# Projections interleaved with the state-space scan, keys turned in place, and a shared key copy in a one-core decoder layer

## The chip, the cores and the metric

The kernel runs on one core of a Trainium2 chip. The metric is the device time of one execution in microseconds (us). The kernel before took 1406.85 us (median of 3 runs, 1405.76 to 1408.14).

## The reference

One decoder layer on two inputs at once: a prompt of 256 tokens and 8 samples of 4 new tokens with a cache of 1024 positions. Everything is float32. Cut to what matters here:

```python
h = rmsnorm(x, norm_mix)
q, k, v, z, dt_raw, xbc = split(h @ w_in)            # 1024 -> 3080 columns
q, k = rope(rmsnorm(q)), rope(rmsnorm(k))            # 8 heads of 64
att = dilated_attention(q, k, v)                     # prompt: own keys; samples: cached keys and values too
u = silu(causal_conv(xbc, conv_w) + conv_b)          # width 4
xs, b_in, c_in = split(u)
dt = softplus(dt_raw + dt_bias)
y, h_last = ssd_scan(xs, dt, -exp(a_log), b_in, c_in, h0)   # chunks of 128 tokens, 8 heads
y = rmsnorm((y + xs * d_skip) * silu(z))
x = x + concat(att, y) @ w_out
x = x + memory_attend(rmsnorm(x), mem_k, mem_v) @ w_mem_o
x = x + moe_ffn(rmsnorm(x))                          # 32 experts, top 4, 12 MB of weights each
```

## The kernel before

It is one program of five instruction streams (TensorE, VectorE, ScalarE, GpSimd, and SyncE, which issues most transfers). Each stream is written out in order by hand, and streams meet only at named semaphores; nothing is reordered. So an engine that waits holds back all that stands behind it in its stream.

The 288 tokens are three row tiles: t = 0 and 1 are the prompt's halves (128 rows each), t = 2 is the 32 sample rows. Weights and caches come through a ring of six slots of 2 MB (`UNITS` assigns the slot, unit number modulo 6; `freed` says which semaphore frees it). SyncE loads the units in list order and waits for each slot in turn.

TensorE's stream up to the experts has these stages, each finished before the next begins:

1. Projections (L362 q, k, v, z for both halves, each into a bank of its own; L369 the samples; L377 dt; L389 the eight column tiles of xbc). ScalarE copies the results, VectorE norms and ropes q and k, then convolves xbc (L1104, L1106).
2. Prompt attention: q and k turned (L399, L407), the scores (L426), softmax on VectorE and ScalarE (L1144 to L1153, L1650), the probabilities turned (L463) and the values weighed (L474).
3. The scan, chunk by chunk: scores of the chunk (L511), decay sums (L517), initial states turned (L497), the part within a chunk (L544), the chunk's state (L552), and on the other engines the decay matrix (L1206, L1208 on VectorE, its exponential L1683 on ScalarE, L1212 on VectorE) and y (L1218 to L1241). GpSimd scales the initial states (L1890). Then the new sample states (L568, VectorE L1259), the norm of y and its turning (L582).
4. Window attention of the samples, in two batch groups g of four batches. For each pair of batches (bb) ten key tiles are turned (L601) into three banks and copied by ScalarE into `KTB` (L1699), and the scores run in two column groups of the array (L622). Then softmax, the probabilities turned (L629), the values weighed (L642), the rows selected (L648).
5. The output projection w_out (L662, L667), then the memory keys and values (L690, L704), memory attention and its projection, and the router, which ends at about 459 us. The expert loop follows: 32 experts through the same ring.

Stages 1 to 5 up to L704 are what the change touches. A float32 matmul shows as two MATMUL records, a transpose as one.

## Time and profile before

| | |
|---|---|
| median of 3 runs | 1406.85 us |
| the profiled execution's own time | 1409.51 us |
| its span, first to last instruction | 1407.3 us |
| TensorE busy | 1275.6 us, 91% |
| VectorE, ScalarE, GpSimd busy | 343.7, 268.3, 35.0 us |
| bytes read from memory | 463.94 MB |
| mean granted TensorE clock | 0.956 of full |

The page's shares are of the whole run, two thirds of which is the expert loop. What a change before the loop is worth is read from the stretches before it. "Busy" counts a matmul at the clock that was granted, so the same work counts up to twice as long at the lower of the two clock levels (1.2 and 2.4 GHz; a clock of 0.50 is all 1.2 GHz).

### The profile page before, as it was taken

Reading aid. Unit: us, or ns where it says so; the run is one execution under the profiler, and the core shown is the slowest. Engines: PE = TensorE matmul, PEld = TensorE weight load, DVE = VectorE, ACT = ScalarE, POOL = GpSimd, SP = SyncE. Lnnn points to the kernel's source line nnn. Section 1 sums busy time; section 2 is a strip of 40 time slices with the busy share of each in tenths; the row PEclk is TensorE's granted clock in tenths of the full one; section 3 lists DMA queues with packets and bytes.
Section 4 is the critical chain, followed back from the end, with each engine's and each line's share of the span. In section 5 each row is a group of like instructions: output and inputs, shape, how many; then the busy total and the mean of one; then the engine's idle time right before and its main releaser. Section 6 shows DMA issues by size and latency. Waiting matters only on the chain.

```text
span 1407.3 us, 15596 instructions
## 1 busy us (share of the span) xinstructions
PE 1275.6 (91%) x6333; PEld 519.7 (37%) x6333; DVE 343.7 (24%) x600; ACT 268.3 (19%) x520; POOL 35.0 (2%) x43
## 2 busy tenths in 40 slices
PE   6998788899778899999999999999999999999997
PEld 3467545344534233333323233232332323323232
DVE  1247550132405212212112121131211312113122
ACT  2126223310422110111102111021110211102111
POOL 0011320000000000000000000000000000000000
PEclk9998768999997899999999999999999999999999
DMA  9251028875028499999999999999999999999995
GB/s 343 103 198 49 0 78 317 312 268 203 12 74 344 154 409 432 426 431 426 431 426 431 426 430 427 430 427 430 427 430 427 430 427 431 426 430 427 430 427 217
DMA packets 54621, 470.19 MB, mean 334 GB/s; under 512 B 6417, under 2 KB 6673, under 8 KB 27972
## 3 DMA queue, kind: packets, MB, share of 16 engines
q1 hardware_dynamic: 52852, 463.69, 79.3%
q0 software_dynamic: 1744, 6.14, 1.4%
q8 instruction: 18, 0.29, 0.1%
q14 instruction: 7, 0.06, 0.0%
HBM read 463.94 MB, written 5.88 MB: 334 GB/s over the span
## 4 chain that ended last, share of the span: by engine, by line
PE 62%; DMA 23%; DVE 8%; ACT 6%; issue 1%; SPq 0%; ACTq 0%; DVEq 0%
DMA ring<-in_w_gate_up 23%; PE PS L913 22%; PE PS L945 10%; PE PS L893 5%; PE PS L362 4%; PE PS L662 3%; PE PS L389 2%; PE PS L704 2%; PE PS L622 1%; PE PS L716 1%; ACT arena L1699 1%; PE PS L642 1%; DVE arena L1503 1%; DVE arena L1505 1%; DVE arena L1500 1%
## 5 line engine op out<-in xcount | busy, mean ns | idle before, releaser
L913 PE MATMUL PS<-ring,arena 128*64 128x512 f32 x1792 | 406.2, 596 | 38.6 <-DMA ring<-in_w_gate_up 37.8
L913 PEld LDWEIGHTS PS<-ring,arena 128*64 128x64 f32 x1792 | 125.8, 137 | 307.1 <-issue 233.2
L945 PE MATMUL PS<-ring,arena 128*64 128x512 f32 x1024 | 230.3, 597 | 5.6 <-ACT arena L1817 5.6
L1500 DVE TENSOR_SCALAR arena<-PS 128x512 f32<-128x512 f32 x32 | 22.1, 692 | 425.9 <-PE PS L913 425.9
L1814 ACT ACTIVATE arena<-arena 128x512 f32<-128x512 f32 x32 | 20.1, 629 | 522.6 <-DVE arena L1500 522.6
L945 PEld LDWEIGHTS PS<-ring,arena 128*64 128x64 f32 x1024 | 69.3, 137 | 132.7 <-issue 118.8
L1466 DVE TENSOR_TENSOR X<-X,PS 128x1024 f32<-128x1024 f32 x34 | 41.5, 1221 | 272.2 <-PE PS L893 272.2
L872 PE MATMUL PS<-arena 128*64 128x512 f32 (+1 forms) x396 | 97.5, 610 | 2.2 <-issue 2.2
L893 PE MATMUL PS<-arena 128*64 128x512 f32 x340 | 81.3, 592 | 1.4 <-ACT arena L1824 1.4
L1824 ACT COPY arena<-PS 64x512 f32<-64x512 f32 x64 | 37.1, 580 | 158.5 <-PE PS L945 158.1
L362 PE MATMUL PS<-ring,arena 128*128 128x512 f32 x128 | 56.9, 607 | 1.1 <-DVE arena L1028 1.1
L913 PE MATMUL PS<-arena 128*64 128x512 f32 x256 | 57.6, 592 | 0.0
L872 PEld LDWEIGHTS PS<-arena 128*64 128x64 f32 (+1 forms) x396 | 25.7, 137 | 67.7 <-issue 67.7
L893 PEld LDWEIGHTS PS<-arena 128*64 128x64 f32 x340 | 24.4, 137 | 50.1 <-issue 50.1
L662 PE MATMUL PS<-ring,mixT 128*128 128x512 f32 x96 | 41.7, 594 | 0.0
L362 PEld LDWEIGHTS PS<-ring,arena 128*128 128x128 f32 x128 | 24.8, 194 | 32.5 <-issue 31.3
L837 PE MATMUL PS<-arena 32*64 32x512 f32 x264 | 36.8, 627 | 0.0
L1470 DVE TENSOR_TENSOR X<-PS,X 32x512 f32<-32x512 f32 x34 | 23.2, 682 | 49.4 <-PE PS L893 49.1
L389 PE MATMUL PS<-arena,ring 128*128 128x288 f32 x128 | 33.0, 422 | 0.0
L913 PEld LDWEIGHTS PS<-arena 128*64 128x64 f32 x256 | 18.4, 137 | 36.5 <-issue 36.5
L704 PE MATMUL PS<-ring,arena 128*128 128x512 f32 x64 | 27.7, 593 | 1.5 <-DVE arena L1331 1.5
L1796 ACT COPY arena<-PS 128x512 f32<-128x512 f32 x33 | 19.4, 587 | 47.8 <-PE PS L872 47.8
(325 smaller groups left out, 1028.4 us busy)
## 6 DMA issues: line engine op xcount, KB each, us to landing
ring<-in_w_gate_up SPq DMA_DIRECT2D x112, 2048.0 KB, 24.8
ring<-in_w_down SPq DMA_DIRECT2D x64, 2048.0 KB, 22.5
arena<-in_w_gate_up SPq DMA_DIRECT2D x16, 2048.0 KB, 27.6
ring<-in_w_in SPq DMA_DIRECT2D x6, 2048.0 KB, 17.0
ring<-in_cache_win_k SPq DMA_DIRECT2D x8, 1024.0 KB, 6.9
ring<-in_cache_win_v SPq DMA_DIRECT2D x8, 1024.0 KB, 10.4
ring<-in_w_out SPq DMA_DIRECT2D x2, 2048.0 KB, 13.7
ring<-in_cache_mem_k SPq DMA_DIRECT2D x4, 1024.0 KB, 7.8
```

Of the source, the lines that this page charges most:

```text
L362: last = mm(PS[:, 2 * g + t, :], hT[:, k, t * P:(t + 1) * P], w[:, k, :], start=k == 0, stop=k == KT - 1)
L389: last = mm(PS[:, bank, 0:NTOK], w[:, k, m % 4 * P:(m % 4 + 1) * P], hT[:, k, :], start=k == 0, stop=k == KT - 1)
L662: last = mm(PS[:, 2 * t + half, :], lhs[:, k, t * P:(t + 1) * P], w(k), start=k == 0, stop=k == nk - 1)
L704: last = mm(PS[:, MKV_BANKS[n], :], HMT[:, k, t * P:(t + 1) * P], w[:, k, :], start=k == 0, stop=k == KT - 1)
L837: last = mm(PS[64 * half:64 * half + 64, nb, :], EROW[r, :], BGU[r, half * 512:(half + 1) * 512], start=True, stop=False, tile_position=(N ...
L872: last = mm(PS[64 * half:64 * half + 64, 2, :], SEL[0:m, t, :], XN[0:m, t, half * 512:(half + 1) * 512], start=t == 0, stop=t == 2, tile_p ...
L893: last = mm(PS[64 * part:64 * part + 64, banks[half], :], SW[:, at:at + 64], YB[:, half, :], start=True, stop=True, tile_position=(0, 64 * ...
L913: last = mm(PS[64 * half:64 * half + 64, nb, :], XT[:, k, :], w[:, k % 2, c:c + 512], start=False, stop=k == KT - 1, tile_position=(0, 64 ...
L945: last = mm(PS[64 * half:64 * half + 64, 5, :], AT[:, k % 4, 64 * (k // 4):64 * (k // 4) + 64], w[:, k % 4, half * 512:(half + 1) * 512], ...
L1466: v.tensor_tensor(x, x, PS[0:n, b:b + 2, :], ALU.add).then_inc(sem("scatter_added"), 1)
L1500: v.tensor_scalar(G1.rearrange("q (c b p) -> q c b p", **by_part), gu[:, 0], 7.0, None, ALU.min).then_inc(sem("gate_ready"), 1)
L1824: ins = s.copy(YB[64 * odd:64 * odd + 64, half, :], PS[64 * half:64 * half + 64, 5, :])
```

## The change

- **Order of loads and projections.** xbc is loaded and projected first, then dt, then the samples of q, k, v, z. The eight prompt outputs of z, q, k, v (`project`, into banks 0 and 1 in turn) are cut into pieces of 2 to 8 matmuls, and the scan's steps stand between the pieces. On VectorE the convolution comes first, the scan next, the norms of q and k after it. ScalarE and GpSimd follow the same order.
- **Prompt attention** stands after the scan, and the first 20 key tiles of the window attention stand between its steps.
- **Keys in place.** A turned key tile is copied back over its own place in the ring slot, so `KTB` is gone; a group's scores run for all four batches at once, in four column groups. Keys are turned through two banks instead of three.
- **Odd key tiles of the second group** (n = 21, 23, ..., 39) are copied by VectorE, the even ones by ScalarE.
- **w_out.** Its four prompt halves stand between the steps of the window attention, and the memory rows are loaded to another place.
- Values go to the arena (`VA`) instead of the ring; SyncE's order is now the list `LOADS`. XD is no longer a tile of its own: the inputs of the scan are scaled in place.

The first place: TensorE's stream from the projections to the first chunk of the scan. `ring,arena 128x512` rows at L362 (before) and L423 (after) are q, k, v, z; `arena,ring 128x288` is xbc; `CN,ring 128x128` at L492 turns an initial state. Before:

```order
L362 MATMUL PS<-ring,arena 128x512 x64
L369 MATMUL PS<-ring,arena 32x512 x32
L377 MATMUL PS<-WDT,arena 128x8 x16
L377 MATMUL PS<-WDT,arena 32x8 x8
L389 MATMUL PS<-arena,ring 128x288 x64
L399 MATMUL PS<-CN,arena 128x128 x16
```

After, the piece from the first chunk's decay sums on:

```order
L477 MATMUL PS<-mixT,CN 128x512 x2
L492 MATMUL PS<-CN,ring 128x128 x4
L423 MATMUL PS<-ring,arena 128x512 x2
L492 MATMUL PS<-CN,ring 128x128 x4
L423 MATMUL PS<-ring,arena 128x512 x2
L492 MATMUL PS<-CN,ring 128x128 x4
L423 MATMUL PS<-ring,arena 128x512 x2
L492 MATMUL PS<-CN,ring 128x128 x4
L524 MATMUL PS<-arena,mixT 128x64 x8
L533 MATMUL PS<-arena 128x256 x2
L423 MATMUL PS<-ring,arena 128x512 x2
```

The 64 projection matmuls that stood in one row now stand in pieces between the scan's steps.

The second place: TensorE in the window attention. Before, the first pair of batches and what follows the second pair:

```order
L601 MATMUL PS<-CN,ring 128x128 x40
L622 MATMUL PS<-arena 32x512 x8
L622 MATMUL PS<-arena 32x128 x8
L622 MATMUL PS<-arena 32x32 x8
L629 MATMUL PS<-CN,arena 128x128 x5
L629 MATMUL PS<-CN,arena 32x128
L642 MATMUL PS<-ring,arena 32x512 x20
```

After (L656 turns keys, L711 scores, L749 is w_out, L722 turns the probabilities, L736 weighs the values):

```order
L711 MATMUL PS<-ring 32x512 x16
L711 MATMUL PS<-ring 32x128 x16
L711 MATMUL PS<-ring 32x32 x16
L749 MATMUL PS<-ring,mixT 128x512 x8
L722 MATMUL PS<-CN,ring 128x128 x5
L722 MATMUL PS<-CN,ring 32x128
L749 MATMUL PS<-ring,mixT 128x512 x8
L736 MATMUL PS<-arena,ring 32x512 x24
L742 MATMUL PS<-CN,ring 128x16 x4
L749 MATMUL PS<-ring,mixT 128x512 x8
L656 MATMUL PS<-CN,ring 128x128 x80
```

A quarter of w_out now stands behind the scores, ahead of each step that waits for the softmax.

The third place: ScalarE between the samples' outputs and the scan. After (L1752 keeps a prompt output, L1759 is silu of z, L1761 to L1764 the scan's exponentials, L1772 keeps a turned state, L1778 is the exponential of the decays):

```order
L1752 COPY arena<-PS 128x512 x2
L1759 ACT_TABLE_LOAD
L1759 ACTIVATE arena<-arena 128x512 x2
L1759 ACTIVATE arena<-arena 32x512
L1761 ACT_TABLE_LOAD
L1761 ACTIVATE small<-small 128x24
L1762 ACTIVATE small<-small 128x24
L1763 ACTIVATE small<-PS 128x8
L1764 ACTIVATE small<-PS 128x32
L1772 COPY ring<-PS 128x512 x2
L1778 ACTIVATE mixT<-mixT 128x1024
L1772 COPY ring<-PS 128x512 x2
```

The first kept state stands behind both prompt outputs of z.

The core of the diff:

```diff
-UNITS = (["q", "k", "v", "z", "xbc0", "xbc1", "h0", "scratch"]
...
+UNITS = ["z", "q", "k", "v", "xbc0", "xbc1",
+         "K0", "K1", "K2", "K3", "h0", "scratch",
...
+LOADS = ("xbc0 xbc1 z q k v h0 K0 K1 wout1 K2 K3 V0 V1 V2 V3 wout0 K4 K5 K6 K7 V4 V5 V6 V7 "
+         "wmk wmq mem0 mem1 wmv mem3 mem2 wmo").split()
...
+            chunk_scores(0)
+            for c in range(4):
+                turn_state(c)
+                if c < 3:
+                    project(2, 2 * c, 2 * c + 2)
+            within(0)
+            chunk_state(0)
+            project(2, 6, KT)
+            chunk_scores(1)
...
+            carried(1)
+            within(1)
+            chunk_state(1)
+            project(3, 6, KT)
+            chunk_scores(2)
+            project(4, 0, 5)
+            carried(2)
+            within(2)
+            project(4, 5, KT)
...
+            def turn_keys(n):
...
+                if n % 20 >= 2 and n < 20:
+                    pe.wait_ge(sem("kt_kept"), n - 1)
+                elif n % 20 >= 2 and n % 2 == 0:
+                    pe.wait_ge(sem("kt_kept"), 20 + (n - 20) // 2)
+                elif n % 20 >= 2:
+                    pe.wait_ge(sem("kt_kept_by_vector"), (n - 21) // 2)
...
+            for n in range(10):
+                turn_keys(n)
+            turn_probs(0, (0, 1))
+            for n in range(10, 14):
+                turn_keys(n)
...
+            weigh_values(0, 2)
+            turn_probs(1, (3, 6, 7, 0))
+            for n in range(14, 18):
+                turn_keys(n)
+            weigh_values(1, 1)
+            for n in range(18, 20):
+                turn_keys(n)
...
+            window_scores(0)
...
+            project_half(mixT, 8, wout[0], 0, WOUT_BANKS[0][0], "mixed_ready")
+            turn_window_probs(0)
...
+            project_half(mixT, 8, wout[1], 0, WOUT_BANKS[0][1], "mixed_ready")
+            weigh_window(0)
+            project_half(mixT, 8, wout[0], 1, WOUT_BANKS[1][0], "mixed_ready")
+            for n in range(20, 40):
+                turn_keys(n)
+            window_scores(1)
+            project_half(mixT, 8, wout[1], 1, WOUT_BANKS[1][1], "mixed_ready")
+            turn_window_probs(1)
+            weigh_window(1)
...
+            for n in range(21, 40, 2):
+                dve.wait_ge(sem("kt_turned"), n + 1)
+                v.tensor_copy(slot(f"K{n // 5}", 5, 512)[:, n % 5, :],
+                              PS[:, KT_BANKS[1][n % 2], :]).then_inc(sem("kt_kept_by_vector"), 1)
...
+            for n in range(5):
+                keep_keys(n)
+            prompt_exp(0)
+            for n in range(5, 10):
+                keep_keys(n)
+            prompt_exp(1)
...
+                if name == "V0":
+                    sp.wait_ge(sem("h_updated"), 8)
+                    sp.wait_ge(sem("y_turned_kept"), 3)
+                    sp.wait_ge(sem("qk_normed"), 3)
+                    sp.wait_ge(sem("prompt_state_stored"), 16)
+                elif name == "V4":
+                    sp.wait_ge(sem("att_rows_ready"), 1)
```

## Rows read from the trace of the kernel before

**Rows 1.** The front by stage (us from the start): busy us of each engine, TensorE clock, DMA.

```profile
core 0: us, PE busy (x) PEld busy (x) DVE busy (x) ACT busy (x) POOL busy (x), PEclk, DMA share, GB/s
15.60:79.50 63.90, 63.90 (x193) 26.86 (x193) 13.08 (x22) 7.30 (x13) 0.00 (x0) 0.97 0.48 173
...
117.30:147.60 30.30, 22.83 (x175) 20.25 (x175) 23.15 (x42) 19.68 (x65) 6.45 (x10) 0.77 0.14 47
147.60:182.40 34.80, 26.56 (x152) 18.53 (x152) 23.36 (x26) 7.84 (x15) 16.48 (x8) 0.75 0.00 1
182.40:202.90 20.50, 16.10 (x30) 6.21 (x28) 13.37 (x21) 2.77 (x5) 3.32 (x3) 0.53 0.11 30
202.90:240.50 37.60, 30.90 (x240) 18.68 (x240) 3.52 (x10) 13.51 (x26) 0.00 (x0) 0.85 0.81 290
240.50:277.60 37.10, 30.40 (x240) 17.94 (x238) 3.08 (x8) 12.26 (x25) 0.00 (x0) 0.86 0.84 326
277.60:312.20 34.60, 33.16 (x146) 15.72 (x145) 7.66 (x15) 5.59 (x12) 0.95 (x1) 1.00 0.71 256
312.20:421.20 109.00, 89.12 (x449) 49.38 (x450) 29.18 (x52) 29.58 (x74) 3.04 (x5) 0.92 0.30 108
```

**Rows 2.** The chain that ended last: start us, us, what (a matmul counts twice).

```profile
15.60 56.90 PE PS L362 x128
72.50 7.01 PE PS L369 x64
79.50 4.27 PE PS L377 x48
83.77 32.94 PE PS L389 x128
...
130.62 4.03 ACT arena L1650 x16
...
152.93 0.96 ACT arena L1683
153.92 1.24 DVE arena L1212
...
312.23 27.70 PE PS L704 x64
```

**Rows 3.** TensorE in time order: start us, us, operation, idle before and releaser.

```profile
187.67 10.61 PE L568 MATMUL PS<-arena 32*128 32x512 f32 x12 [2.50 <-DVE ring L1259]
...
210.57 4.75 PE L622 MATMUL PS<-arena 128*32 128x512 f32 x48 [0.81 <-ACT arena L1699]
215.25 4.92 PE L601 MATMUL PS<-CN,ring 128*128 128x128 f32 x40
...
228.96 1.54 PE L629 MATMUL PS<-CN,arena 128*128 128x128 f32 x6 [3.21 <-ACT arena L1702]
```

**Rows 4.** TensorE groups kept apart by shape, 0 to 340 us: busy us, mean ns.

```profile
L622 PE MATMUL PS<-arena 128*32 128x512 f32 x64 | 14.5, 595 | 3.2 <-ACT arena L1699 3.2
```

**Rows 5.** ScalarE in time order: the copies of ten turned key tiles.

```profile
215.94 4.99 ACT L1699 COPY arena<-PS 128x512 f32<-128x512 f32 x10 [5.43 <-PE PS L601]
```

**Rows 6.** VectorE in time order: one operation, in chunk 0 and in chunk 1.

```profile
155.06 0.68 DVE L1218 TENSOR_TENSOR arena<-arena,RP 128x512 f32<-128x512 f32 x1
...
168.86 2.38 DVE L1218 TENSOR_TENSOR arena<-arena,RP 128x512 f32<-128x512 f32 x1
```

**Rows 7.** GpSimd in time order, at chunk 1.

```profile
165.96 9.33 POOL L1890 TENSOR_TENSOR ring<-ring,small 128x1024 f32<-128x1024 f32 x4 [13.97 <-PE PS L497]
```

**Rows 8.** Transfers: GB/s in 40 slices; by kind the median us to landing.

```profile
GB/s 343 103 198 49 0 78 317 312 268 203 12 74 344 154 409 432 426 431 426 431 426 431 426 430 427 430 427 430 427 430 427 430 427 431 426 430 427 430 427 217
...
ring<-in_cache_win_v SPq DMA_DIRECT2D x8, 1024.0 KB, 10.4
...
out_ssm_sample<-ring POOLq DMA_DIRECT2D x1, 2048.0 KB, 10.9
```

**Rows 9.** The chain near the end of the run.

```profile
1355.59 24.80 DMA ring<-in_w_gate_up
```

More of the change, by code:

```diff
@@ L56, in slot_loads @@
 def slot_loads(upto, slot):
-    return sum({"s": 0, "p": 0, "K": 2, "V": 2, "m": 2}.get(UNITS[i][0], 1) for i in range(slot, upto, RING))
+    return sum({"s": 0, "p": 0, "K": 2, "m": 2}.get(UNITS[i][0], 1) for i in range(slot, upto, RING))
 def constants():
@@ L500, in _ @@
-            H0T = slot("scratch", NB, 512)
-            for t in range(3):
+            project(0, 0, KT)
+            turn_xb(0)
+            turn_xb(1)
+            pe.wait_ge(sem("dta_ready"), 1)
+            for c in range(3):
+                n = ROWS[c]
+                tri = cst("tri") if c < 2 else cst("tri_s")
+                tot = cst("ones") if c < 2 else cst("same_s")
+                mm(PS[0:n, 6, CUM + c * 8:CUM + c * 8 + 8], tri, DTA[0:n, c, :], start=True, stop=True)
+                mm(PS[0:n, 6, CUM + 32 + c * 8:CUM + 40 + c * 8], tot, DTA[0:n, c, :], start=True, stop=True)
@@ L504, in _, with chunk_scores @@
+            pe.wait_ge(sem("drep_ready"), 1)
+            for p in range(4):
+                last = mm(PS[:, 6, CUM + 64 + 8 * p:CUM + 72 + 8 * p],
+                          DREP[0:NTS, 2 * p:2 * p + 2, :].rearrange("p h d -> p (h d)"), cst("bsel"),
+                          start=True, stop=True)
+            last.then_inc(sem("cumulated"), 1)
+            project(1, 0, 4)
+            turn_xb(2)
+            project(1, 4, KT)
+            def chunk_scores(t):
                 n = ROWS[t]
@@ new lines, in _ @@
+            chunk_scores(0)
[7 more added lines that the diff above has]
+            chunk_scores(1)
+            for c in range(4):
+                turn_state(4 + c)
+                if c < 3:
+                    project(3, 2 * c, 2 * c + 2)
+            carried(1)
+            within(1)
+            chunk_state(1)
+            project(3, 6, KT)
@@ new lines, in turn_qk @@
+            def turn_qk(t, banks):
+                pe.wait_ge(sem("qk_normed"), t + 2)
+                for j in range(2):
+                    for p in range(4):
+                        last = nc.tensor.transpose(PS[:, banks[j], p * P:(p + 1) * P],
+                                                   QK[:, t, j, 2 * p:2 * p + 2, :].rearrange("p h d -> p (h d)"),
+                                                   ident)
+                    last.then_inc(sem("qk_turned"), 1)
+            project(6, 0, 4)
@@ new lines, in _ @@
+            pe.wait_ge(sem("state_rows_kept"), 1)
+            turn_qk(0, (2, 3))
+            project(6, 4, KT)
+            project(7, 0, 4)
+            turn_y(0)
+            turn_y(1)
+            project(7, 4, 6)
+            turn_y(2)
+            add_states(0)
+            project(7, 6, KT)
+            add_states(1)
+            add_states(2)
+            add_states(3)
+            pe.wait_ge(sem("proj_kept"), 11)
+            for j in range(2):
+                r = slice(32 * j, 32 * j + 32)
+                for p in range(4):
+                    last = nc.tensor.transpose(PS[:, j, p * NTS:(p + 1) * NTS],
+                                               QKS[r, 2 * p:2 * p + 2, :].rearrange("p h d -> p (h d)"),
+                                               ident[r, r])
@@ new lines, in _ @@
+            for c in (6, 7):
+                silu_conv(c, slice(0, SEQ), c + 1)
+            for c in range(8):
+                silu_conv(c, slice(SEQ, NTOK), 9)
+            act.wait_ge(sem("proj_ready"), 1)
+            s.copy(QKS[0:64].rearrange("p h d -> p (h d)"), PS[0:64, 7, :]).then_inc(sem("proj_kept"), 1)
+            s.copy(V[0:NTS, 2, :], PS[64:96, 7, :]).then_inc(sem("proj_kept"), 1)
+            s.copy(Z[0:NTS, 2, :], PS[96:128, 7, :]).then_inc(sem("proj_kept"), 1)
+            root_heads(64, AH, DH)
@@ new lines, in _, with keep_qk @@
+            s.copy(HOUT, PS[:, 2, :].rearrange("p (c n) -> p c n", c=4)).then_inc(sem("state_rows_kept"), 1)
+            act.wait_ge(sem("y_gated"), 3)
+            square_y(2)
+            root_heads(P, 2 * AH, DH)
+            act.wait_ge(sem("y_squared"), 3)
+            root(RS, SSQ, 512)
+            keep_projected(5)
+            root_heads(P, 2 * AH, DH)
+            def keep_qk(t, banks):
+                for j in range(2):
+                    act.wait_ge(sem("qk_turned"), 3 * t + j + 1)
+                    s.copy((qT, kT)[j][:, :, t * P:(t + 1) * P],
+                           PS[:, banks[j], :].rearrange("p (c n) -> p c n", c=4)).then_inc(sem("qk_kept"), 1)
@@ L1654, in _, with keep_probs @@
-            for i in range(2):
+            def keep_probs(i, banks):
                 act.wait_ge(sem("probs_turned"), i + 1)
-                banks = (2, 3, 5, 6)
                 for j in range(i + 1):
```

1080 lines of the change are left out of this document (550 added, 530 removed).

## The prediction

> **What bounds the kernel now.** I read the stretches by stage first, then the chain that ended last, then each engine in order of time where the chain leaves TensorE.
>
> Near the end of the run the chain is a weight transfer of 24.80 us for the experts [rows 9], and from slice 15 on the memory delivers a steady 426 to 432 GB/s [rows 8]. The expert loop is paced by its 12 MB per expert, and the change does not touch it. But it can't run ahead: an expert's slots are freed by the expert before, so the whole loop starts when the front is done. Any time won before L704 moves everything behind it by as much, since that work (109.0 us to the projection of the memory attention, then the router) is the same before and after [rows 1].
>
> In the front, from 15.60 (first projection) to 312.23 (first matmul of the memory keys) [rows 2], the chain is TensorE's nearly throughout the projections, then changes engine every microsecond or two. From 117.3 to 202.9 (prompt attention and scan) TensorE is busy 65.5 of 85.6 us, and at a granted clock of only 0.77, 0.75 and 0.53; from 202.9 to 277.6 (window attention) 61.3 of 74.7 us at 0.85 [rows 1]. The projections and w_out run at 0.97 to 1.00 with hardly any idle. So the front is a dense part, a part that waits, another that waits and a dense part, and the change lays them over each other. What this can give is read from TensorE's work, and what stays is its waits.
>
> **TensorE's work in the new order.** I sum it at the full clock.
>
> - Projections: 56.90 + 7.01 + 4.27 + 32.94 = 101.1 us [rows 2]; same work, other order.
> - Prompt attention and scan: 22.83 x 0.77 + 26.56 x 0.75 + 16.10 x 0.53 = 46.0 us [rows 1]. The conversion is fair where matmuls are long: six state updates (L568, x12) took 10.61 us, 1.77 each for 512 columns [rows 3], against 0.889 for a 512-column projection (56.90 / 64) [rows 2]. That is half clock.
> - Window attention: 30.90 x 0.85 + 30.40 x 0.86 = 52.4 us [rows 1]. The scores now use four column groups instead of two. With two, 32 matmuls of 512 columns took 14.5 us, 0.453 each [rows 4]; with four, the samples' projection took 7.01 / 32 = 0.219 each [rows 2]. 32 x 0.234 = 7.5 us go. I count nothing for the 128- and 32-column ones. Leaves 44.9.
> - w_out and the turned memory rows: 33.2 us, at clock 1.00 [rows 1].
>
> Sum 225.2 us. Before, the same stretch took 312.2 - 15.6 = 296.6. If TensorE never waited and kept its clock, 71.4 us would go.
>
> **The waits that stay.** For these I followed the four streams through the new order with the durations of the trace.
>
> - First projection: xbc0 and xbc1 take the places in the load order that q and k had, and TensorE showed no idle there before [rows 1]. Now all of z, q, k, v must be there at 15.6 + 32.9 + 4.3 = 52.8 us. The loads up to there are 343 GB/s x 35.2 us = 12.1 MB in the first slice and 3.6 MB more in the second [rows 8]; at the first slice's rate these are in by 46 us. No wait; if I am wrong, a few us.
> - Chunk 0 of the scan, 3 us. ScalarE keeps the second output of z, does its silu and the scan's exponentials before it keeps the first turned state, so the second state is turned 1.7 us late. Then the decay (0.96 us on ScalarE, 1.24 on VectorE [rows 2], and the two passes before them) is ready about 1.3 us after the pieces of projection run out. In the old order nothing stood beside this chain.
> - Chunks 1 and 2, 2 us, of the same kind.
> - GpSimd beside VectorE: in chunk 1 the same VectorE operation took 2.38 us where it took 0.68 in chunk 0 [rows 6], and GpSimd scaled the initial states in four pieces of 9.33 us in all just then [rows 7]. After the change this scaling comes again when all eight states are turned, beside chunk 1. Some 4 us of VectorE are lost, now mostly beside 5 matmuls of `project(4)`; I leave 1 us on the path (within the 2 below); all 4 if that cover is gone.
> - End of the scan (y's norm, second norm of q and k, state updates): 2 us.
> - Prompt attention with the first 20 keys: here ScalarE sets the pace. 20 key copies at 0.50 (4.99 / 10 [rows 5]) are 10.0 us, and with two banks instead of three each waits for its tile to be turned (0.49, from 4.92 / 10 [rows 3]), which makes them some 0.6: 12. Exponentials 4.03 us for the second half [rows 2], by its size some 3.4 for the first; six copies of probabilities and two of outputs, 4. With the maximum and the reductions that the first of them waits for, I get 30 us from the prompt scores to the last key. TensorE's own work in it is 18.5. So 11.5 us of wait: the largest item.
> - Keys 20 to 39: two banks, two engines. A bank's round is a turn of 0.49, a copy of 0.59 to 0.69 and the handing over, 1.24 for two tiles, 0.62 a tile against 0.49: 2.5 us. ScalarE alone on two banks would also need 0.6, so the share of VectorE is worth about nothing on the path (from -1 to +2 us): it halves the load of ScalarE, but the banks bind. Nobody else waits for VectorE there; the residual's first half is done before.
> - Window outputs and the hand-over to the memory rows: 7 us. The softmax of each group, for which TensorE waited 3.21 us [rows 3], goes behind a w_out half of 6.9 us (27.7 / 4). What stays is the selected rows (two waits of about 0.9), and the end: VectorE norms the memory rows ahead of the samples' residual, and ScalarE starts their squares only after the last window output.
>
> Sum: 3 + 2 + 2 + 11.5 + 2.5 + 7 = 28 us. New stretch: 225.2 + 28 = 253.2; saved 296.6 - 253.2 = 43.4 us. The profiled execution took 1409.5, so 1366.1 by its scale; from the median 1406.85 it is 1363.5. I take 1363.5.
>
> Transfers behind the front: the values V0 to V3 now wait for the state updates (about 155 us) and are wanted at about 208; a value load landed 10.4 us after issue and the samples' state took 10.9 us to be stored [rows 8], ahead of w_out's first half wanted at about 193. Both have tens of us of room. Keys 4 to 7 are freed by the first scores and wanted 30 us later. I cost all at nothing.
>
> **A rule weighed.** The Trainium skill ("SBUF — State Buffer", section "Who interferes with whom") says that a VectorE instruction with two inputs in SBUF and a GpSimd instruction that reads SBUF shut each other out for a whole instruction. The row of 2.38 us agrees. By that rule any scan step can be held for one GpSimd piece, 9.33 / 4 = 2.3 us, and the new order puts more of VectorE's scan beside GpSimd's masks and scaling; taken at five such hits, none covered, the sum would be 11.5 us less gain. I count it in the range.
>
> **Rivals.**
>
> 1. *The pieces cover nearly all, the clock stays full* (15 in 100). ScalarE's stage costs 4 instead of 11.5 and the ends 3 instead of 7: 1363.5 - 11.5 = 1352. For it: TensorE then never idles for more than a microsecond or two. Against: 24 us and more of ScalarE work in that stage.
> 2. *The scan's chain sets the pace* (20 in 100). Each projection output is kept by ScalarE in line behind the scan's copies and exponentials, and with two banks only, a late copy stops the projections. If TensorE fell to half clock for a third of the 57 us of projections (+19), it is 1363.5 + 19 = 1382. If only the window part won (109.3 before, 44.9 + 33.2 + 9.5 after, 21.7 saved), 1385.
> 3. *Slower: the clock is lost* (4 in 100). The dense projections are cut into pieces of 2 to 5 matmuls with waits between them. From 182.4 to 202.9 TensorE was busy 16.1 of 20.5 us and yet at 0.53 of its clock [rows 1]. Were the 56.9 us of projections all to run at the lower level they would cost 57 us more: 1420. It turns into a loss once more than 43 of the 57 us are lost, three quarters of them. Against it: the 277.6 to 312.2 stretch holds 1.00 with a little idle.
> 4. *No change* (1 in 100): the front would have to be hidden behind transfers; slices at 0 and 12 GB/s say otherwise [rows 8].
>
> **How the numbers follow.** The forecast has 60 in 100: 1354 to 1375. The range of 8 in 10 reaches to the scan-paced case and to the packed one: 1350 to 1382. This measurement can tell some 0.2%, 3 us, from no change. Faster by more: 60 + 15 + 20 = 95; same 1; slower 4.
>
> **What would show it.** In the new profile the first matmul of the memory keys (L801) starts at about 269 us (15.6 + 253.2) instead of 312. The clock between 60 and 155 us is above 0.9, and the projection pieces take 0.89 us a matmul. TensorE waits for ScalarE's key copies for some 10 us between about 158 and 188. Key tiles 20 to 39 come at 0.6 us. The scores of one group take 5 to 6 us, once per group. The experts' part is as long as before. I am wrong if the projection pieces show the half clock, if TensorE waits for projection outputs to be kept, or if it waits for a transfer before 310 us.

## The result, and the profile after

The changed kernel took 1370.5 us (median of 4 executions, 1366.86 to 1374.6) against 1406.7 for the kernel before on the same chip: a ratio of 0.9743, with an interval of 0.9708 to 0.9778, or 36.2 us less. Forecast were 43.4 less (1363.5 us). Its eight executions, four here and four in the next comparison, fall into two groups: two at 1366.9 and 1367.7, with a mean granted clock of 0.973 and 0.974, and six between 1373.3 and 1375.0, at 0.968 or 0.969. What probably divides them is told below; the profiled execution, at 1374.6, belongs to the longer ones, and none of the two shorter ones was profiled.

First the front by stage, the rows that answer to [rows 1]. 15.7 is the first projection, 82.1 the scan's first matmul, 161.5 the prompt's scores, 198.6 the first window scores, 232.2 key tile 20, 247.2 the second window scores, 277.2 the first matmul of the memory keys.

```profile
core 0: us, PE busy (x) PEld busy (x) DVE busy (x) ACT busy (x) POOL busy (x), PEclk, DMA share, GB/s
15.70:64.20 48.50, 48.50 (x250) 34.78 (x250) 18.48 (x45) 13.87 (x40) 2.92 (x11) 0.93 0.79 273
64.20:82.10 17.90, 17.90 (x73) 9.98 (x72) 12.17 (x29) 4.75 (x8) 4.33 (x5) 1.00 0.03 7
82.10:125.30 43.20, 39.93 (x201) 22.94 (x200) 25.42 (x31) 14.83 (x28) 15.08 (x8) 1.00 0.08 31
125.30:161.50 36.20, 36.20 (x104) 16.43 (x102) 22.39 (x39) 8.26 (x18) 4.24 (x6) 0.88 0.60 211
161.50:198.60 37.10, 26.25 (x185) 22.21 (x184) 12.36 (x17) 23.30 (x61) 2.47 (x2) 0.75 0.75 283
198.60:232.20 33.60, 32.67 (x206) 14.24 (x207) 4.27 (x10) 1.84 (x5) 0.00 (x0) 1.00 0.61 240
232.20:247.20 15.00, 11.34 (x81) 8.43 (x80) 6.92 (x10) 5.86 (x10) 0.00 (x0) 1.00 0.40 166
247.20:277.20 30.00, 26.35 (x255) 12.92 (x255) 9.43 (x21) 7.44 (x17) 0.95 (x1) 0.94 0.81 286
sum 261.50, PE 239.15 PEld 141.93 DVE 111.45 ACT 80.14 POOL 30.00; mean PE 29.89 PEld 17.74 DVE 13.93 ACT 10.02 POOL 3.75
```

Read the last line first: the front takes 261.5 us where it took 296.6, so 35.1 are saved, and the profiled executions differ by 34.9 (1409.5 and 1374.6). Nothing was won or lost behind it. TensorE is busy for 239.15 of the 261.5 us and idle for 22.35. Busy time by the granted clock of each row (48.50 x 0.93 and so on) is 223.3 us of work at the full clock; the other 15.9 us of busy time are the price of the lower clock. The fourth and fifth rows hold 10.9 of them, and the fourth has no idle time at all.

Then TensorE in order of time, at three places. First the scan's first chunk (start us, us, operation, idle before and releaser):

```profile
84.21 0.60 PE L492 MATMUL PS<-CN,ring 128*128 128x128 f32 x4
84.65 1.88 PE L423 MATMUL PS<-ring,arena 128*128 128x512 f32 x4
88.14 0.66 PE L492 MATMUL PS<-CN,ring 128*128 128x128 f32 x4 [1.61 <-ACT ring L1772]
88.63 1.88 PE L423 MATMUL PS<-ring,arena 128*128 128x512 f32 x4
```

L423 is a piece of a projection, L492 the turning of an initial state. A piece of two matmuls takes 1.88 us and stands where TensorE would wait for ScalarE's copy of the state; 1.61 us of wait stay ahead of the second state.

Second the end of the scan and the prompt's attention, which answers to the state updates of [rows 3]:

```profile
149.27 3.02 PE L574 MATMUL PS<-arena 32*128 32x512 f32 x6
...
154.34 7.19 PE L574 MATMUL PS<-arena 32*128 32x512 f32 x8
161.47 5.21 PE L635 MATMUL PS<-arena 64*128 64x128 f32 x32
...
175.57 2.91 PE L656 MATMUL PS<-CN,ring 128*128 128x128 f32 x12 [4.31 <-ACT ring L1834]
...
184.52 1.97 PE L656 MATMUL PS<-CN,ring 128*128 128x128 f32 x8 [3.54 <-ACT ring L1834]
...
193.79 1.15 PE L656 MATMUL PS<-CN,ring 128*128 128x128 f32 x8 [1.76 <-ACT ring L1834]
```

The last four state updates (L574, two records each) take 7.19 us, 1.80 each, with no idle time in front: half clock, as before the change (1.77 each, there behind a wait of 2.50 us). Three updates just ahead of them took 3.02, 1.0 each. In the attention TensorE waits for ScalarE's copies of key tiles (L1834), 4.31, 3.54 and 1.76 us.

Third the window scores, which answer to L622 in [rows 3, 4], and key tiles 20 to 39:

```profile
198.64 4.81 PE L711 MATMUL PS<-ring 128*32 128x512 f32 x96 [0.73 <-ACT ring L1834]
203.38 7.13 PE L749 MATMUL PS<-ring,mixT 128*128 128x512 f32 x16
...
238.47 1.09 PE L656 MATMUL PS<-CN,ring 128*128 128x128 f32 x8 [0.34 <-DVE ring L1451]
239.91 1.09 PE L656 MATMUL PS<-CN,ring 128*128 128x128 f32 x8 [0.35 <-DVE ring L1451]
```

All scores of a batch group are one pass of 4.81 us, with a quarter of w_out (L749) behind it while the softmax runs. The key tiles come in pairs, 1.44 us from one pair to the next, 0.72 a tile; nearly every pair waits for a copy by VectorE.

### The profile page after: what moved, and what is told of

The parts are those of the page before. It is cut to its first block, busy times and chain, and to the rows that moved or that the text cites. A ratio compares the mean times of both kernels' runs of the same rounds, so it can differ in the third digit from the quotient of the medians.

```text
span 1372.5 us, 15591 instructions
## 1 busy us (share of the span) xinstructions
PE 1255.4 (91%) x6333; PEld 512.3 (37%) x6333; DVE 351.3 (26%) x616; ACT 264.9 (19%) x510; POOL 33.4 (2%) x43
## 4 chain that ended last, share of the span: by engine, by line
PE 64%; DMA 24%; DVE 6%; ACT 5%; issue 1%; SPq 0%; ACTq 0%; DVEq 0%
DMA ring<-in_w_gate_up 23%; PE PS L1009 23%; PE PS L1041 10%; PE PS L989 5%; PE PS L423 4%; PE PS L749 3%; PE PS L395 3%; PE PS L801 2%; PE PS L813 1%; PE PS L656 1%; DVE arena L1635 1%; DVE arena L1637 1%; DVE arena L1632 1%; PE PS L1030 1%; ACT arena L1998 1%
## 5 line engine op out<-in xcount | busy, mean ns | idle before, releaser
L423 PE MATMUL PS<-ring,arena 128*128 128x512 f32 x128 | 58.1, 596 | 0.0
L749 PE MATMUL PS<-ring,mixT 128*128 128x512 f32 x96 | 42.4, 596 | 0.0
L656 PE MATMUL PS<-CN,ring 128*128 128x128 f32 x160 | 24.6, 299 | 13.0 <-ACT ring L1834 10.3
L395 PE MATMUL PS<-arena,ring 128*128 128x288 f32 x128 | 36.2, 450 | 0.0
L423 PEld LDWEIGHTS PS<-ring,arena 128*128 128x128 f32 x128 | 23.1, 190 | 23.7 <-issue 23.2
L395 PEld LDWEIGHTS PS<-arena,ring 128*128 128x128 f32 x128 | 27.1, 214 | 8.3
## 6 DMA issues: line engine op xcount, KB each, us to landing
ring<-in_w_down SPq DMA_DIRECT2D x64, 2048.0 KB, 22.4
```

The source lines that it names most:

```text
L395: last = mm(PS[:, XBC_BANKS[m], 0:NTOK], w[:, k, m % 4 * P:(m % 4 + 1) * P], hT[:, k, :], start=k == 0, stop=k == KT - 1)
L423: last = mm(PS[:, i % 2, :], hT[:, k, t * P:(t + 1) * P], w[:, k, :], start=k == 0, stop=k == KT - 1)
L656: last = nc.tensor.transpose(PS[:, KT_BANKS[g][n % 2], p * P:(p + 1) * P], K[:, j, p * P:(p + 1) * P], ident)
L749: last = mm(PS[:, bank, :], lhs[:, k, t * P:(t + 1) * P], w[:, k, :], start=k == 0, stop=k == nk - 1)
```

## The experiments

Twelve runs were made in three comparisons, each comparison on a chip of its own. Times are medians of four executions (five for the last kernel) and ratios are to the kernel before on the same chip. "The 128-row kernel" is that of the first experiment; from the second comparison on it is the base of all edits, since its times form one group.

| kernel | us | ratio (interval) |
|---|---|---|
| changed kernel again | 1374.3 | 0.9768 (0.9752 to 0.9785) |
| state updates over 128 rows | 1366.2 | 0.9709 (0.9692 to 0.9725) |
| pieces of projection last | 1389.7 | 0.9877 (0.9861 to 0.9894) |
| w_out last | 1378.6 | 0.9812 (0.9790 to 0.9835) |
| 128 rows again | 1365.6 | 0.9712 (0.9689 to 0.9735) |
| 128 rows, ScalarE copies keys 20 to 39 | 1363.0 | 0.9686 (0.9662 to 0.9710) |
| 128 rows, four banks | 1359.9 | 0.9672 (0.9649 to 0.9695) |
| 128 rows, VectorE copies keys 10 to 19 | 1367.4 | 0.9716 (0.9690 to 0.9743) |
| 128 rows, scores in two passes | 1379.3 | 0.9786 (0.9763 to 0.9808) |
| 128 rows, dt projection spread | 1365.4 | 0.9693 (0.9673 to 0.9713) |
| 128 rows, four banks, ScalarE copies | 1358.7 | 0.9639 (0.9619 to 0.9659) |
| 128 rows, four banks, keys 10 to 19, dt spread | 1358.0 | 0.9624 (0.9599 to 0.9649) |

**The clock at the state updates.** The changed kernel ran again beside a kernel that contracts the updates over 128 rows (GpSimd clears both operands beforehand, so the rows 32 to 127 add zeros).

> The changed kernel again, unedited, on the same chip: 1367 to 1375 us, the memory keys' projection starts within 3 us of 277.2, the clock falls again at the state updates. Theory A (its spread of 8 us comes from the clock, which is given up at different moments) expects a start of the projection that moves with the time; theory B (the spread is in the expert loop) a start within 0.5 us of 277.2 and a different length behind it.

```diff
-                mm(PS[:, 4 + n % 2, :], XDE[0:NTS, 2, p * P:(p + 1) * P],
-                   BNM[0:NTS, p // 2, 4 * half:4 * half + 4, :].rearrange("p b n -> p (b n)"),
+                mm(PS[:, 4 + n % 2, :], XDE[:, 2, p * P:(p + 1) * P],
+                   BNM[:, p // 2, 4 * half:4 * half + 4, :].rearrange("p b n -> p (b n)"),
```

> The eight state updates (L574) contract over 128 rows instead of 32; the 96 added rows are zeros, so the result is the same, and two memsets on GpSimd clear them. Theory A (the clock was given up because these matmuls use a quarter of the array's rows): the clock from 150 to 165 us stays near 1.00 instead of 0.76, 0.50, 0.50, the last four updates take 3.5 us instead of 7.1, the prompt scores 3 instead of 5.1, and the memory keys' projection starts 4 to 7 us earlier than 277.2. Theory B (the clock falls for another reason, such as the short work around them): the updates take 7.1 us as before, the start stays within 1 us of 277.2. By both the GpSimd memsets cost nothing, since the updates' input is ready some 25 us ahead.

The changed kernel took 1374.3 us, all four executions in the longer group, and its memory keys start at 277.5. So both of its profiles are of long executions, and they can't show by themselves where the short ones gain. The 128-row kernel took 1366.2 us: 8.1 less. TensorE by stretches of 5 us, first in the changed kernel, then in the 128-row kernel:

```profile
core 0: us, PE busy (x), PEclk, DMA share, GB/s
150.00:155.00 5.00, 5.00 (x22) 0.76 0.81 218
155.00:160.00 5.00, 5.00 (x7) 0.50 0.87 306
160.00:165.00 5.00, 5.00 (x26) 0.50 0.32 75
```

```profile
150.00:155.00 5.00, 5.00 (x25) 1.00 0.86 238
155.00:160.00 5.00, 5.00 (x38) 1.00 0.96 310
160.00:165.00 5.00, 3.96 (x28) 1.00 1.00 316
```

Both are busy throughout up to 160; the one falls to half clock, the other does not. It then does in 1.09 us what took 1.92 (L594, q and k of the prompt's second half turned), in 3.79 what took 7.19, and in 2.89 what took 5.2 (the prompt's scores). The first key tile comes at 159.9 instead of 166.6, the memory keys at 270.0 instead of 277.2. But one profile alone would mislead: the kernel with w_out last keeps the 32 rows, and its profiled execution did not fall either.

```profile
152.37 3.88 PE L574 MATMUL PS<-arena 32*128 32x512 f32 x8
156.18 2.89 PE L635 MATMUL PS<-arena 64*128 64x128 f32 x32
```

So the 128-row kernel was run again as the base of three others.

> The kernel with the state updates contracted over 128 rows once more, as the base of the three others of this comparison. The profiled run of the changed kernel had TensorE at a granted clock of 0.50 from 155 to 165 us with no idle time, while it did the last state updates over 32 rows; the kernel with 128 rows had 1.00 there, but so had the kernel with w_out behind the window attention, which keeps the 32 rows. Theory A (the 32 rows make the clock fall, in most executions but not in all): four more executions at 1364 to 1367.5 us and 1.00 in the profile from 145 to 163 us. Theory B (the fall is chance, whatever the rows): about half of the executions 6 to 8 us longer than the others, at 1371 to 1375 us.

It took 1365.6 us (1365.1 to 1367.3). Over all profiles of this study the four last updates took 7.19 us in three of the four with 32 rows (3.88 in the fourth), and 3.79 in all nine with 128 rows. The 128-row times (1364.4 to 1367.3) lie at and just below the shorter group of the changed kernel (1366.9, 1367.7). So the fall costs about 7 us, it comes with the 32 rows in most executions and not in all, and in no profile with 128 rows. That the shorter group is the executions without it fits their granted clock, but no profile shows it. That it is the rows and not the changed moment of the clearing or of the waits was not separated either.

**The pieces of projection.** The three outputs whose pieces stood between the scan's steps (q and k of the prompt's first half, q of the second) go behind the scan as one row; the expectation calls them q, k and v.

```diff
                 turn_state(c)
-                if c < 3:
-                    project(2, 2 * c, 2 * c + 2)
...
+            project(2, 0, KT)
+            project(3, 0, KT)
+            project(4, 0, KT)
             project(5, 0, KT)
```

> The prompt projections of q, k and v stand in one row behind the scan's chunks instead of in pieces between its steps. Theory A (the pieces hide the scan's chain of VectorE and ScalarE steps): the three chunks are exposed as in the kernel before, where they took 34.8 us; with the 18 us of pieces that stood beside them this is 53 us instead of the 40 of the changed kernel from the first chunk's scores to the end of the third: 1 to 2 us less for nothing, so the memory keys' projection starts 10 to 15 us later than 277.2, and the clock in the scan falls to about 0.75. Theory B (most of the gain came from the window part): at most 4 us later.

1389.7 us against 1374.3: the interleaving is worth 15.4 us, and both have the fall at the state updates (7.19 us). In the profiles the memory keys start 17.0 us later (294.4 for 277.5 in the changed kernel of this comparison); 10 to 15 were expected. The same chunk 0 without the pieces:

```profile
84.21 0.60 PE L492 MATMUL PS<-CN,ring 128*128 128x128 f32 x4
88.14 1.11 PE L492 MATMUL PS<-CN,ring 128*128 128x128 f32 x4 [3.33 <-ACT ring L1767]
89.93 1.12 PE L492 MATMUL PS<-CN,ring 128*128 128x128 f32 x4 [0.68 <-ACT ring L1767]
93.34 1.12 PE L492 MATMUL PS<-CN,ring 128*128 128x128 f32 x4 [2.29 <-ACT ring L1767]
94.25 3.62 PE L524 MATMUL PS<-arena,mixT 128*128 128x64 f32 x16
```

and the whole scan, without the pieces and then, in the changed kernel, with them:

```profile
82.00:123.80 41.80, 31.42 (x153) 0.65 0.09 32
```

```profile
82.00:125.30 43.30, 40.03 (x201) 1.00 0.08 31
```

Without the pieces the scan takes 41.8 us at a clock of 0.65 (the expectation had 0.75), which is 31.42 x 0.65 = 20.4 us of work; with them 43.3 at 1.00, so 40.03 - 20.4 = 19.6 us of projection cost 1.5 us. Of the other 18.1 us 7.1 lie in waits that they fill (10.4 idle against 3.3), and 11.0 us are the half clock that they avoid (31.42 - 20.4): the part within a chunk, L524, takes 1.97 with them and 3.62 without. The 18.1 are of one pair of profiles and of this stretch; the medians show 15.4. Rival 2 feared the opposite, that the scan would take the projections' clock.

**w_out beside the window softmax.** The four quarters of w_out go behind the window attention.

```diff
             window_scores(0)
-            pe.wait_ge(sem("att_kept"), 2)
-            loaded("wout0")
-            project_half(mixT, 8, wout[0], 0, WOUT_BANKS[0][0], "mixed_ready")
             turn_window_probs(0)
...
+            for t in range(2):
+                for half in range(2):
+                    loaded(f"wout{half}")
+                    project_half(mixT, 8, wout[half], t, WOUT_BANKS[t][half], "mixed_ready")
```

> The four prompt halves of w_out stand behind both groups of the window attention instead of between its steps; their residual additions follow. Theory A (they hide the softmax and the loads): TensorE waits again about 3.2 us for each group's softmax and 1 us for the probabilities, twice: 7 to 10 us later than 277.2, and the clock in the window part falls below 0.9, which may add 2 to 4 us. Theory B (the window part gains only by the four column groups and the keys in place): at most 2 us later.

1378.6 us (1375.0 to 1383.5) against 1374.3 for the changed kernel in the same comparison: 4.3 slower in the medians. The profiled execution, 1375.0, had no fall at the state updates, so it is better held against the changed kernel at 1366.9 and 1367.7 or the 128-row kernel at 1366.2, some 7 to 9 us. The waits are back:

```profile
198.02 1.31 PE L721 MATMUL PS<-CN,ring 128*128 128x128 f32 x6 [3.20 <-ACT ring L1877]
200.31 7.86 PE L735 MATMUL PS<-arena,ring 128*32 128x512 f32 x48 [0.98 <-ACT ring L1882]
```

3.20 us of softmax are uncovered for each batch group, as in [rows 3], and the window outputs behind it take 7.86 and 7.32 us instead of 5.49, at a lower clock: 6.4 + 4.2 = 10.6 us. From the first window scores to the memory keys the profiles show 89.3 us for 78.5, 10.8 more. The execution's time shows less of it, because it came to those scores with less clock lost: it had no fall at the state updates, and half of the usual one near 36 us (told below).

**The score pass.** The 96 matmuls of a score pass in two passes over two column groups each.

```diff
-                for part in range(3):
-                    for p in range(4):
-                        for b in range(4):
+                for bb in range(2):
+                    for part in range(3):
+                        for p in range(4):
+                            for b in (2 * bb, 2 * bb + 1):
```

> On top of the 128 rows, the window scores of a batch group run as two passes over two column groups each instead of one pass over four. The 96 matmuls of a pass took 4.81 us in the changed kernel. Theory A (matmuls in different column groups overlap, so the count in one pass doesn't matter beyond the number of groups): each of the two score stretches rises from 4.8 to about 8.5 to 9.6 us, and the kernel is 7.5 to 9.6 us slower than the 128-row kernel, at 1373 to 1376 us. Theory B (the stretch is bounded by the waits around it, the window softmax behind it on ScalarE and VectorE): most of it is taken up by the window outputs, which wait 1 us or less in between, and the kernel is 0 to 3 us slower.

1379.3 us, on another chip than its base (1365.6), so the ratios are compared: 0.9786 against 0.9712, some 10 us; the profiled spans differ by 13.7. The scores of a batch group take

```profile
189.62 9.22 PE L712 MATMUL PS<-ring 128*32 128x512 f32 x96 [0.73 <-ACT ring L1836]
```

9.22 us instead of 4.81, both at a clock of 1.00, so 8.8 us for the two groups, and nothing of it is hidden. (The prediction had counted 7.5 us for the four column groups.) The memory keys start 9.1 us later (278.5 for 269.4): a quarter of w_out took 1.7 us more (8.81 for 7.11), and the window scores had started 1.3 us sooner. The other 4.6 us of the span lie behind them, where both kernels do the same work: by that much one execution differs from another there.

**The copies of key tiles 20 to 39: the titled part.** Two edits, by themselves and together: ScalarE copies all twenty tiles, as before the change; and the tiles go through four banks instead of two.

```diff
-            for n in range(20, 40, 2):
+            for n in range(20, 40):
                 keep_keys(n)
```

> On top of the 128 rows, ScalarE copies all twenty key tiles of the second batch group, as before the change. Theory A (two banks pace the turning: turn 0.55, copy 0.59 to 0.69 and two hand-overs of 0.2 to 0.35 each make 1.43 us for two tiles, whoever copies): the twenty tiles still take 14 to 15 us, the kernel's time within 1 us of the 128-row kernel. Theory B (the copying engine paces: one engine copies 20 tiles at 0.59 and waits 0.26 for each, 0.85 a tile): 17 us in place of 14.4, the kernel 2 to 3 us slower.

```diff
-        KT_BANKS = ((4, 5), (0, 1))
+        KT_BANKS = ((4, 5), (0, 1, 4, 5))
...
+                elif n == 22:
+                    pe.wait_ge(sem("residual_ready"), 1)
+                elif n >= 24 and n % 2 == 0:
+                    pe.wait_ge(sem("kt_kept"), 20 + (n - 22) // 2)
```

> On top of the 128 rows, the twenty key tiles of the second batch group go through four PSUM banks instead of two. Theory A (two banks pace the turning): the pace falls from 0.72 us a tile to that of the transposes alone, 0.52 to 0.55, so 3.4 to 4 us less over the twenty, and the kernel at 1362 to 1363 us. Theory B (copies and hand-overs by two engines pace it, or what is saved is waited for later, at the window scores or the window outputs): the stretch stays at 14 us or the time within 1 us of the 128-row kernel.

> On top of the 128 rows, four banks for the key tiles of the second batch group, and ScalarE alone copies them. With two banks ScalarE alone took 13.2 us for the twenty tiles, both engines 14.2; with four banks both engines took 8.9 us. Theory A (with four banks the copying engine paces): 20 copies of 0.54 us one after the other, 11 us, so 2 us slower than four banks with two engines, at 1361.5 to 1363 us: that is what VectorE's half is worth once the banks don't pace. Theory B (TensorE's transposes pace at 0.45 us): about 9 us for the twenty and the same time as four banks with two engines, 1360 us.

From the first of the twenty tiles to the start of the scores, in the profiles:

| | both engines copy | ScalarE alone |
|---|---|---|
| two banks | 15.0 us | 13.9 us |
| four banks | 9.7 us | 10.6 us |

```profile
232.51 1.12 PE L652 MATMUL PS<-CN,ring 128*128 128x128 f32 x8 [0.21 <-ACT ring L1826]
233.81 1.16 PE L652 MATMUL PS<-CN,ring 128*128 128x128 f32 x8 [0.18 <-ACT ring L1826]
```

```profile
224.97 8.90 PE L658 MATMUL PS<-CN,ring 128*128 128x128 f32 x80
```

The first fence is ScalarE alone on two banks: TensorE waits 0.2 us for a bank, where it waits 0.35 for VectorE's. With two banks the round of a bank binds, and the engine with the longer copy makes it longer (0.69 us a tile for VectorE, 0.59 for ScalarE): VectorE's help costs 1.1 us. The 15.0 is the same within 0.03 us in all nine profiles with two banks and both engines; the other three cells are one profile each. With four banks (second fence) TensorE turns all twenty tiles without a wait, at 0.45 us each, and VectorE's help is worth 0.9. The times of the two four-bank kernels don't show the 0.9: 0.9672 with both engines, 0.9639 with ScalarE alone, intervals that overlap. So the title's edit was undone at no loss (1363.0 against 1365.6 us, intervals that overlap), and the missing part of it is the banks: 5.7 us in the medians, 5.3 in the stretch.

**ScalarE's stage in the prompt's attention.** VectorE copies key tiles 10 to 19.

```diff
+                for n in ((10, 11, 12, 13), (14, 15, 16, 17, 18, 19))[i]:
+                    turned_key(n)
...
-            for n in range(10, 14):
-                keep_keys(n)
```

> On top of the 128 rows, VectorE copies key tiles 10 to 19 of the first batch group, which ScalarE copies between the exponentials and the attention's copies. Theory A (ScalarE paces the prompt's attention: TensorE waits 4.3, 3.5 and 1.8 us for it there): ScalarE has 10 x 0.54 = 5.4 us less, of which the wait of 3.5 us before the third piece and that of 1.8 us give back 2 to 4 us; the kernel at 1362 to 1364.5 us. Theory B (the softmax chain itself paces, exponentials, probabilities and turns, and the keys only fill its gaps): within 1 us of the 128-row kernel, or up to 1 us slower since a VectorE copy takes 0.69 where ScalarE's takes 0.59.

The stage did what the first theory says: from the first key tile to the window scores 27.7 us (160.5 to 188.2) instead of 31.6 (159.3 to 190.9). The time did not: 1367.4 against 1365.6. 3.9 us were won there. In the profiles 1.2 had gone before it began, 1.6 went at a quarter of w_out

```profile
214.87 8.75 PE L751 MATMUL PS<-ring,mixT 128*128 128x512 f32 x16
```

(7.11 in the base) and 3.2 behind the front, where the work is the same (the span less the start of the memory keys is 1097.5 for 1094.3); in the first 100 us from the memory keys on the clock was 0.88 where the base had 0.91. The slow quarter of w_out needs no VectorE copies of these tiles: the kernel with the scores in two passes has it too (8.81 us). Whether the copies cause the loss behind the front, or it differs from one execution to the next, stays open.

**The dt projection.** The clock also falls near 36.5 us, in the changed kernel for some 7 us, 3 us after 24 matmuls with 8 output columns began (33.2 to 37.9). It does so in all eleven profiles in which they stand in one row (0.79 over 32 to 48 us in nine of them, 0.89 in two), and it did before the change, right behind the same matmuls (0.59 from 83.8 to 88.0 us). They were spread over three places.

```diff
-                if m == 4:
...
+                if 2 <= m < 5:
...
+                    t = m - 2
```

> On top of the 128 rows, the 24 small matmuls of the dt projection (eight output columns each) are spread: eight ahead of each of the third, fourth and fifth blocks of the convolved channels, instead of all ahead of the fifth. In every trace so far the granted clock falls to 0.50 from about 36.5 to 43 us, 3 us after these matmuls start, with TensorE busy throughout. Theory A (a row of small matmuls makes the clock fall): no fall, 3.3 us less by the time of the first projection, the kernel at 1361.5 to 1363.5 us. Theory B (the fall has another cause at that time, such as the transfers that saturate the DMA engines until 46 us): the same fall, and the time within 1 us of the 128-row kernel.

The same 10 us in the 128-row kernel, and then with the spread projection:

```profile
35.00:40.00 5.00, 5.00 (x33) 0.56 1.05 387
40.00:45.00 5.00, 5.00 (x17) 0.76 1.05 376
```

```profile
35.00:40.00 5.00, 5.00 (x35) 1.00 1.05 387
40.00:45.00 5.00, 5.00 (x23) 1.00 1.06 381
```

The fall is gone in both profiles with the spread projection, with the transfers unchanged, so these transfers alone don't cause it; the prompt's scores start 2.9 us sooner (153.5 for 156.5) and the memory keys 3.0 (266.4 for 269.4). The median does not show it: 1365.4 us, ratio 0.9693 against 0.9712 with intervals that overlap. The profiled execution was the fastest of its four (1362.9, at a mean clock of 0.978; the others 1365.0 to 1366.4 at 0.973 to 0.976), so it shows what can be won and not what is won each time. The last kernel, with the same spreading, shows one way in which it can be lost: no fall at 36 us, but one at 72 to 76, right behind the small matmuls of the decay sums, and its scores start at 156.2.

```profile
71.95 5.40 PE L424 MATMUL PS<-ring,arena 128*128 128x512 f32 x8
```

(3.70 in the changed kernel.)

**All together.** 128 rows, four banks with both engines copying, key tiles 10 to 19 by VectorE, the dt projection spread.

> All that promised something: state updates over 128 rows, four banks for the second group's key tiles with both engines copying, VectorE copying key tiles 10 to 19 of the first group, and the dt projection spread. Each by itself at full clock: 5.3 us for the banks, 3.9 us for the copies (taken back in part by the clock in the kernel that had it alone), 3.3 us for the spread projection if the clock stays up. Theory A (the clock stays up while TensorE idles less): 1366 - 5.3 - 3.9 - 3.3 = 1353.5, so 1352 to 1356 us. Theory B (what is saved in waits is partly taken back by the clock behind it, as with the copies alone): 1357 to 1361 us.

1358.0 us (1352.4 to 1359.8), ratio 0.9624: 50.5 us less than the kernel before in the same comparison, where the changed kernel, with ratios of 0.9743 and 0.9768, saved 32 to 36. The parts add up to 1353.5, and only two of five executions came near it (1352.4, 1353.8); three lie at 1358 to 1360, where the second theory has them. It can't be told from the 128-row kernel with four banks and ScalarE alone (0.9639). Not run by themselves were the first twenty key tiles between the steps of the prompt's attention, and the keys kept in place.

## Why the prediction was right, and where it was off

- **The mechanism held.** The memory keys start at 277.2 us instead of 312.2, and the tail is as long as before. The forecast was 269. TensorE waits for no transfer before them. Undoing the interleaving costs 15.4 us, undoing w_out's place some 8, and undoing the four column groups some 9.
- **Work at the full clock:** 225.2 forecast, 223.3 measured. The forecast was not quite at the full clock: its 101.1 us of projections are busy time as it stood, 63.90 us at 0.97 [rows 1] and 37.20 at 0.95 (the row below, dt and xbc before the change), which is 97.3 at the full clock. So 3.8 us of clock loss were in the sum unnamed, and the work by itself came out 1.9 above 221.4. The scores take 4.81 us a group, the pieces 0.94 us a matmul when short and 0.87 to 0.88 in long rows.

```profile
79.50:117.30 37.80, 37.20 (x177) 29.45 (x176) 16.64 (x42) 13.78 (x34) 4.41 (x12) 0.95 0.56 192
```

- **Waits:** 28 forecast, 22.4 measured. By place: scan 5 and 3.3; end of the scan 2 and none; prompt's attention 11.5 and 10.9; keys 20 to 39 2.5 and 3.7; window outputs and hand-over 7 and 4.6. The largest was right by its cause as well: the copies taken off ScalarE shortened its stage by 3.9. A part of what is missing in the waits is the clock's doing: in two kernels in which TensorE turned the probabilities ahead at full clock (L664, 1.2 us for 1.84), it then waited some 4.15 us for ScalarE before key tiles 12 and 13, and not 3.54.
- **The clock is the term that was mis-sized.** The step was "I sum it at the full clock": beside the waits the sum has no term for a lower clock, and the state updates, seen at half clock in [rows 3], were taken over at the full one with no reason given. Measured are 15.9 us: 3.4 at the dt projection, 4.3 at the state updates, 6.6 in the attention behind them (some 2.3 of it at the prompt's scores, right behind the updates), 1.6 at the samples' projection of w_out. The first two stand in rows without any idle time. [Rows 3] had shown the updates at half clock (six at 1.77 us each in a single group without a gap, behind one wait of 2.50), and [rows 1] the projection stage at 0.97 with no idle time. With +15.9 for it, -5.7 for the waits and -1.9 for the work the stretch is 8.3 us above the forecast: 261.5 for 253.2. That the time still lay 7 us from the forecast owes something to luck: the shorter waits (5.7) and the loss that the sum already held (3.8) hid a good part of the clock's price.
- **The titled copies:** "worth about nothing on the path", between -1 and +2. It came out at a loss of 1.1 in the profiles, just outside, for the reason given: the banks bind. The pace of 0.62 a tile was 0.72, since a bank's round took 1.44 us and not 1.24: a turn of 0.52, VectorE's copy of 0.69, and 0.23 for the two hand-overs (the pair starts at 238.47, VectorE copies from 239.17 to 239.86, the next pair starts at 239.91: 0.18 from the turn to the copy, 0.05 back).
- **The rule weighed.** In chunk 1 GpSimd scales the initial states in four pieces, and VectorE beside it is slower again (the first line is of chunk 0):

```profile
97.94 0.69 DVE L1343 TENSOR_TENSOR arena<-arena 128x512 f32<-128x512 f32 x1
...
110.52 1.75 DVE L1327 TENSOR_TENSOR arena<-arena 128x512 f32<-128x512 f32 x1
112.30 0.69 DVE L1330 TENSOR_TENSOR arena<-arena,PS 128x512 f32<-128x512 f32 x1
113.03 1.54 DVE L1336 TENSOR_TENSOR arena<-arena,small 128x512 f32<-128x512 f32 x1
...
115.21 1.66 DVE L1343 TENSOR_TENSOR arena<-arena 128x512 f32<-128x512 f32 x1
```

```profile
107.97 8.35 POOL L2056 TENSOR_TENSOR ring<-ring,small 128x1024 f32<-128x1024 f32 x4 [6.29 <-PE PS L492]
```

The operations with two inputs in SBUF take 1.75 and 1.54 us, the one that reads PSUM keeps its 0.69. The next with two inputs in SBUF, L1343, takes 1.66 us here and 0.69 in chunk 0, with GpSimd idle. TensorE does not wait for any of it (its only wait between 108 and 121 us is 0.77, for ScalarE); pieces of projection stand beside it. The Trainium skill ("SBUF — State Buffer", section "Who interferes with whom") names this case, and the trace agrees; the 11.5 us which it could have cost did not come.
- **Rivals.** The packed case (1352) is what the last kernel reached at best, with four edits that the change lacks. The scan-paced case is refuted by the profile: beside the scan the pieces ran at a clock of 1.00, and TensorE waited 3.3 us there.

## What to carry to other kernels

Dense matmuls laid between the steps of a chain paid twice here, in the waits that they filled (7.1 us) and in the clock, which stayed up for the chain's own matmuls (11.0). A second engine for copies out of PSUM helped in these profiles only where the banks didn't bind: count the round of a bank (turn, copy, two hand-overs) before splitting the copies, and add banks first. A sum at the full clock needs a term for stretches that were busy and yet below 1.00 in the trace before, and executions that fall into two groups by time call for several profiles before an edit is credited.

## What was unexpected in the hardware

- TensorE at half clock with no idle time: in 155 to 165 us of the changed kernel, during state updates over 32 rows; with the same work over 128 rows it stays at 1.00 in nine profiles of nine.
- With the same code up to there the clock falls in one profile and not in another: from the second turning of q and k (L594) to the first key tile it is 14.1 us in the changed kernel's profile and 7.7 in that of the kernel with w_out last.
- After 24 matmuls of 8 columns the clock was 0.50 for some 6 us in TensorE's next long matmuls, and 1.00 when they were spread in three lots of eight (eleven profiles of eleven, and two of two).
- Two engines that share the copies of two banks were slower than the faster of them alone: 15.0 and 13.9 us for twenty tiles.
